# Two places for weight chunks and one more place in each ring of gathered expert rows

## The reference

```python
mod = silu(c) @ w_ada + b_ada                      # shift, scale, gate, twice
h = rmsnorm(x, g1) * (1 + scale1) + shift1
proj = h @ w_in                                    # q k v u gv gate_a gate_b, 7 x 1024 columns
out_b = stick_breaking_attention(q, k, v)          # 8 heads of 128
out_a = u * chunk_spatial_gate(layernorm(gv))
x = x + gate1 * ((gate_a * (out_a @ w_ba) + gate_b * (out_b @ w_bb)) @ w_out)
h = rmsnorm(x, g2) * (1 + scale2) + shift2
# PEER: 8 heads, the best 16 of 16384 experts each
q = h @ w_query
experts, gates = top16_pairs(q @ sub_keys)         # 8 * 16 experts a token
act = gelu(sum(h * expert_down[experts]))
x = x + gate2 * sum(gates * act * expert_up[experts])
y = rmsnorm(x, g_final)
```

## Time and profile before

| | |
|---|---|
| median of 3 runs | 2391.7 us (2390.11 to 2401.53) |
| profiled execution | 2380.01 us, span 2377.8 us |
| PE, TensorE matmuls | busy 1856.2 us, 78% |
| DVE, VectorE | busy 1558.0 us, 66% |
| POOL, GpSimd | busy 1263.7 us, 53% |
| ACT, ScalarE | busy 559.9 us, 24% |
| moved | 844.90 MB, mean 355 GB/s; 604.05 MB of it gathered |

### The profile page before, as it was taken

How to read it: one execution, slowest core, us unless ns; L and a number is a source line. 1 busy time by engine, 2 the same in 40 slices (tenths; PEclk the granted TensorE clock), 3 DMA queues, 4 the chain that set the end, 5 groups by cost and what they waited for, 6 DMA issues and landing times.

```text
span 2377.8 us, 24899 instructions
## 1 busy us (share of the span) xinstructions
PE 1856.2 (78%) x7896; PEld 1296.7 (55%) x7896; DVE 1558.0 (66%) x3451; ACT 559.9 (24%) x1186; POOL 1263.7 (53%) x1169
## 2 busy tenths in 40 slices
PE   4785879888898786998977999778466567777777
PEld 2555878676777564765754577666344223222232
DVE  1210155778888667776787876767679987676662
ACT  1040021476211122136322310111111212122121
POOL 0000025656665455664676665655467677767773
PEclk7997979888999887999977876989688899999999
DMA  7875879998999889996999999999899999999997
GB/s 265 343 274 161 296 292 362 410 348 291 353 388 410 327 324 364 410 412 250 386 408 409 380 401 361 401 380 351 294 410 333 356 358 410 392 409 409 409 409 268
DMA packets 219009, 844.90 MB, mean 355 GB/s; under 512 B 26495, under 2 KB 35639, under 8 KB 197376
## 3 DMA queue, kind: packets, MB, share of 16 engines
q0 software_dynamic: 165888, 604.05, 65.7%
q1 hardware_dynamic: 36820, 216.87, 24.0%
q10 hardware_dynamic: 16172, 22.39, 2.7%
HBM read 826.16 MB, written 16.80 MB: 355 GB/s over the span
## 4 chain that ended last, share of the span: by engine, by line
PE 38%; DMA 21%; DVE 17%; POOL 7%; issue 7%; DVEq 5%; ACT 3%; SPq 1%; ACTq 0%; POOLq 0%
PE bank L846 11%; DMA gather_ring<-in_expert_down,expert_numbers 9%; PE bank L837 9%; PE bank L1202 7%; DVE gather_ring L1920 4%; DVE expert_sums L1951 4%; DMA gather_ring<-in_expert_up,expert_numbers 4%; DMA weight_chunks<-in_w_in 3%; POOL gather_ring L802 3%; POOL gather_ring L787 3%; PE bank L1126 2%; SPq L693 1%; PE bank L1123 1%; DMA weight_chunks<-in_w_ada 1%; POOL weight_chunks L787 1%
## 5 line engine op out<-in xcount | busy, mean ns | idle before, releaser
L787 POOL DMA_INDIRECT gather_ring<-in_expert_down,expert_numbers x510 | 590.0, 1157 | 778.1 <-DVEq L1883 363.3
L1202 PE MATMUL bank<-gather_ring,coef_diagonals 128*128 128x512 f32 x1040 | 578.7, 698 | 264.6 <-DMA gather_ring<-in_expert_up,expert_numbers 155.9
L802 POOL DMA_INDIRECT gather_ring<-in_expert_up,expert_numbers x532 | 564.0, 1060 | 274.1 <-issue 135.1
L1920 DVE CUSTOM_DVE_ANT_0 gather_ring<-gather_ring,h_tiles 128x1024 f32<-128x1024 f32 x410 | 500.1, 1226 | 187.1 <-DMA gather_ring<-in_expert_down,expert_numbers 167.5
L1202 PEld LDWEIGHTS bank<-gather_ring,coef_diagonals 128*128 128x128 f32 x1040 | 213.8, 219 | 561.3 <-issue 402.1
L846 PE MATMUL bank<-hT,weight_chunks 128*128 128x128 f32 (+2 forms) x2304 | 412.4, 341 | 30.4 <-DVE u_and_gv L1773 9.8
L846 PEld LDWEIGHTS bank<-hT,weight_chunks 128*128 128x128 f32 x2304 | 382.0, 202 | 79.8 <-issue 48.8
L1951 DVE SCALAR_TENSOR_TENSOR expert_sums<-gather_ring,expert_coefs,expert_sums 128x1024 f32<-128x1024 f32 x269 | 345.8, 1285 | 8.6 <-issue 8.6
L837 PE MATMUL bank<-weight_chunks,hT 128*128 128x256 f32 x960 | 219.3, 387 | 18.7 <-DMA weight_chunks<-in_w_in 18.2
L837 PEld LDWEIGHTS bank<-weight_chunks,hT 128*128 128x128 f32 x960 | 185.4, 195 | 54.6 <-DMA weight_chunks<-in_w_in 22.7
L1512 ACT ACTIVATE coef_diagonals<-identity,expert_coefs 128x128 f32<-128x128 f32 x304 | 108.3, 395 | 375.4 <-DVE expert_coefs L1931 178.6
(11 more groups left out here) (266 smaller groups left out, 2055.2 us busy)
## 6 DMA issues: line engine op xcount, KB each, us to landing
weight_chunks<-in_w_in SPq DMA_DIRECT2D x84, 1024.0 KB
weight_chunks<-in_w_ada SPq DMA_DIRECT2D x24, 1024.0 KB
weight_chunks<-in_w_query SPq DMA_DIRECT2D x24, 1024.0 KB
weight_chunks<-in_w_branch_a SPq DMA_DIRECT2D x12, 1024.0 KB
weight_chunks<-in_w_branch_b SPq DMA_DIRECT2D x12, 1024.0 KB
weight_chunks<-in_w_out SPq DMA_DIRECT2D x12, 1024.0 KB
gather_ring<-in_expert_up,expert_numbers POOLq DMA_INDIRECT x532, 11.0
weight_chunks<-in_cache_k SPq DMA_DIRECT2D x16, 512.0 KB
```

The costliest lines, as they stand in the source:

```text
L787: pool.indirect_dma_start(out=d_row(slot), out_offset=None, in_=down, in_offset=bass.IndirectOffsetOnAxis(ap=expert[:, t, h * TOPK + k:h * ...
L802: pool.indirect_dma_start(out=u_row(slot), out_offset=None, in_=up, in_offset=bass.IndirectOffsetOnAxis(ap=expert[:, t, h * TOPK + k:h * T ...
L1202: mm = nc.tensor.matmul(bank[6 + half], diag[:, n % 8, :], u_row(slot)[:, half * 512:(half + 1) * 512], start=(u == PE_TILE[t][0]), stop=( ...
L1920: nc.vector.tensor_tensor_reduce(out=row, in0=row, in1=x, scale=1.0, scalar=0.0, op0=ALU.mult, op1=ALU.add, accum_out=dots[:, m % 2, k:k + ...
```

## The change

`weight_chunks` gets two places instead of three (16 KB a partition instead of 24), `gather_ring` thirteen instead of eleven (52 KB instead of 44): six for down and seven for up rows. The sum stays the same. The late rings keep eight places each; two down rows instead of three lie in `weight_chunks` then, and one up row instead of two in `v_tokens`. All indices, waits and counts follow from the three numbers.

```diff
@@ -90,8 +90,8 @@
-D_EARLY, D_LATE = 5, 8
-U_EARLY, U_LATE = 6, 8
+D_EARLY, D_LATE = 6, 8
+U_EARLY, U_LATE = 7, 8
 LATE = 25
@@ -203,7 +203,7 @@
-NW = 3
+NW = 2
```

## The result

The changed kernel takes 2468.4 us (median of 4 runs, 2461.9 to 2484.9) against 2390.9: slower by 77.5 us, ratio 1.0319, 95% interval 1.0274 to 1.0363. The prediction had 2423 and a range to 2460. The profiled execution took 2468.1 us, with a span of 2465.9.

The account below looks back on a forecast made before the run. First stage bound by alternating weight transfers and products, 345 to 1860 us by DMA. Terms 49.5 + 9 + 5 - 4 - 30 + 2 = +31.5 us on the profiled 2380.0 give 2411.5; the median, 11.7 higher, 2423; range 2398 to 2460.

Parts of the forecast that it names:

- (a): First stage, eight ada chunks alone: the eighth ends at 38.8 us instead of 36.9, +2 us.
- (e): End of front 0: four out chunks +2.1 us; queries lose 0.3 us each behind the first gather, counted as nothing.
- (b): q, k and v of front 0: 8.7 us a pair of w_in and ada chunks, 98 us against 69.5, +28.6.
- (d): Merge of front 0: one chunk fewer ready at the modulation store, then 4.33 us a chunk instead of 3.58, +12.5 us.
- (f): First stage, TensorE's clock falling in idle time: slow w_in chunk in half the pairs, +9 us, ends 0 and 27.
- (c): gv and u of front 0: gv 3 would wait, +3 us, and four u chunks add 1.3, +4.3 us.
- Second stage, two places: Fronts 1 and 2: PE falls about 14 us behind, but DMA is the bound; +5 us, ends 0 and 15.
- rival 2: Front 1: PE becomes the bound, its 14 us of weight waits reach the end; 20 for 5, 2438 us, chance 0.05.
- Second stage, rings: Gathers beside fronts 1 and 2: one more place per ring shortens stretches and shallower dips, -30 us, ends -8 and -60.
- ten stops: Stretches between 353 and 1709 us with DVE held up, 48 us in all; each shortened by at most 2.56 us, 24 together.
- The table B2: Near 1671 us, SP asks for this table behind one query chunk instead of two; -4 us, ends 0 and -7.
- The switch to eight places: At row 400, POOL's up gather waits for row 399's sum instead of row 396's; +2 us, ends 1 and 8.

Follow-up runs that it names:

- w2_busy_pe: Kernel before with two weight places, rings five and six, plus ten extra unread matmuls behind each ada chunk in front 0's q, k, v: 2477.5 us against 2391.7.
- w2_alone: Kernel before with two weight places instead of three throughout, rings left at five and six: 2489.7 us against 2391.7.
- w2_front0_only: Kernel before with two weight places for front 0's 72 chunks, three from chunk 72 on, rings five and six: 2468.7 us against 2391.7.
- w2_later_only: Kernel before with three weight places in front 0, two from chunk 72 on, rings five and six: 2414.6 us against 2393.3.
- rings_4_5: Kernel before with one place less in each gather ring (four and five), three weight places: 2416.6 us against 2391.5.

## Why the prediction was wrong

The direction, and front 0 as the place of the loss, were right; the size was not: 31.5 us forecast, 77.5 measured.

**First stage, steps (a) to (e), 49.5 us: right, some 52 measured.** The eighth ada chunk started at 36.86 us, 1.8 later than in the earlier trace rows, with +2 forecast, in part by luck: the first began at 10.44 us, where the term starts from 14.0. Step (b) without the clock is w2_busy_pe: 99.1 us where I had 98. From the end of u to the end of merge it is 13.0 us more, with 12.5 forecast, and the out chunks cost 2.3 for 2.1. The time from issue to use stayed at 4.9 us, and merge chunks took 4.35 us each against 4.33. The idle time at the store began one product earlier: 31.11 us against 26.26. That row lengthens by the one chunk that no longer lay ready, as (d) had it.

**(f), the clock, 9 us: mis-sized.** It measured 19 us in the change's profile: 16 in the eleven pairs of q, k and v (115.1 us against 99.1 in w2_busy_pe), 1.6 at the twelfth chunk and 1.6 at gv 3. I had let half of the pairs run a slow w_in chunk; all eleven did, at 5.1 to 5.5 us. Each had stood behind 3.6 to 5.1 us of idle time, where the two rows that I weighed, had 2.12 and 2.78 before them, and neither was as long as the 3.9 us that I had worked out for the pair. A row that was as long stood in the trace of before, and I didn't use it. Behind 4.09 us of idle time, with 4.6 us of matmuls ahead of that, the four u chunks took 16.41 us, and the granted clock was 0.69 over the first 5.4 us of them (timeline, then window):

```profile
169.07 16.41 PE L846 MATMUL bank<-hT,weight_chunks 128*128 128x128 f32 x128 [4.09 <-DMA weight_chunks<-in_w_in]
...
169.07:174.50 5.43, 5.43 (x34) 5.43 (x35) 3.21 (x6) 0.28 (x1) 0.00 (x0) 0.69 0.75 317
```

It says that every pair would fall. The Trainium skill, "TensorE: Matmul & The Clock Gate", section on HAM oscillation, has the case (a product shorter than the wait, the half rate at every tile), and by that rule (f) was 27. The trace agrees with it in that each pair fell, though with its ada chunk a pair had 4.8 us of work at the full rate, more than its wait. The 27 was too high: I had priced an ada chunk at the lower clock too, and that part (0.85 of 2.45 us a pair) didn't come. In the rows it takes 1.05 us each time, behind the long chunk.

**gv:** step (c) took waits alone. From the start of gv 0 to the end of u it is 7 us more than before, not 4.3; 1.6 of that is gv 3, a slow chunk now (5.2 us instead of 3.62). gv 0 and the start of u were slow in the kernel before already.

**Second stage, two places, +5 (0 to 15): the step that failed most.** Measured 21 us, by w2_alone against w2_front0_only and by w2_later_only. I said that PE's 14 us of waits would be hidden because DMA is the bound there. PE's waits ahead of weight chunks rose by 43 us, not 14, to 55.0 in 32 waits: 30 more of 1.4 us each, where I had 18 of 0.5 to 1. And a share near 1 is no cover: w2_alone moved 356 GB/s instead of 367 over 475 us, which is 14 us. That was rival 2 (chance 0.05), at the right size. Its way, DVE's front pieces waiting for PE, is not what the rows show, though. From 405 to 1950 us DVE's waits for PE's front results are 70 us in both runs; its waits in all are 359 us in w2_alone and 332 in w2_front0_only, and what rose most is its wait for key scores, ahead of the choice of experts, and one wait for the x rows of the residual, which stand behind the chunks in SP's queue (w2_front0_only first, then w2_alone):

```profile
DVE top_values L1836 <- DMA key_scores<-key_scores: 24.5, 5, 8.2
840.64 0.42 DVE L1808 TENSOR_TENSOR scratch_row<-bank,row_tables 128x256 f32<-128x256 f32 x1 [0.72 <-DMA u_and_gv<-in_x_prompt]
...
DVE top_values L1821 <- DMA key_scores<-key_scores: 39.5, 6, 9.8
850.41 0.42 DVE L1793 TENSOR_TENSOR scratch_row<-bank,row_tables 128x256 f32<-128x256 f32 x1 [7.17 <-DMA u_and_gv<-in_x_prompt]
```

The x rows I had named and put inside the 0 to 15. The wait for key scores varies from profile to profile (11.7 us in rings_4_5 to 34.8 with three places later, 39.5 to 53.6 with two), and that it comes from PE's late queries is my reading; no run shows it.

The queries of front 0 under the first gathers, which (e) put at nothing, were 7 us on PE's path into front 1. They aren't part of the 21: w2_front0_only has two places for them as well, and still takes 2055.4 us from its first gather.

**Second stage, rings, -30 (-60 to -8): about right in size, wrong in mechanism.** It measured 21 and 26 us. I had it from ten stops, each shortened by one event. Not one that I looked at is shorter. My reading of why: ahead of a stop the ring is full in both kernels, so what POOL can still issue is what has been freed, and that doesn't depend on the depth. In the stop of 14 us the rows agree: ahead of the last six gathers before it POOL had waited for a place, 2.52 us with rings of five and six and 4.36 with six and seven. Nor was it DVE that held POOL in this stop, as the prediction had it for all ten, but TensorE's sum of an up row. What the extra place does buy is in the shallow dips, which I had given 6 of my 30 us: DVE's waits for down rows fall from 158.3 to 126.6 us. How much of that reaches the end isn't shown.

**The table B2, -4: right in order, no gain to be seen.** In the profile after, the table is asked for behind one query chunk and DVE waits 1.50 us for it, not 4.52, but the stop at the second norm of front 2 lasts about as long as before (9 us at a share of 0.16, 8 at 0.13 before), for DVE waited 8.90 us for the sample tile's tables behind it, and 9.13 before:

```profile
1777.05 1.22 DVE L1810 TENSOR_TENSOR h_tiles<-h_tiles,row_tables 128x1024 f32<-128x1024 f32 x1 [1.50 <-DMA row_tables<-mod_prompt]
...
1790.11 1.28 DVE L1808 SCALAR_TENSOR_TENSOR h_tiles<-u_and_gv,norm_stats,row_tables 128x1024 f32<-128x1024 f32 x1 [8.90 <-DMA row_tables<-mod_sample]
```

**The switch to eight places, +2: right.** POOL waits 3.34 us for the sum of row 399, where the earlier trace rows show 0.30:

```profile
1994.16 0.94 POOL L802 DMA_INDIRECT gather_ring<-in_expert_up,expert_numbers  x1 [3.34 <-PE bank L1202]
```

Put together by what each term measured: 77 + 21 - 26 comes to 72 us, against 77.5. (With the 21 us that the rings gave beside two places it is 77 by construction, and proves nothing.) No single term takes the sum out of the range, which ended 69 us above the median before: with the clock at its end of 27 and the second stage at its end of 15 the sum would be 59.5. But the 21 us of the second stage lie beyond its end, the rings gave 21 to 26 and not 30, the table's 4 us aren't to be seen, and front 0 cost 77 and not 58.5. All these misses went the same way.

## What to carry to other kernels

A prefetch place is worth what its load takes from issue to use, less the other places' work. Here a load took 4.9 us and a product 3.7, so two places passed two chunks in 8.7 us where their products take 7.2, and a pair of a long and a short chunk in 8.7 where its products take 4.8; the idle time in between let TensorE's clock fall as well, and a pair took 10.3. Ask for each buffer in which stage it is scarce: here the ring lay idle just where weight places were short, and lending it (six places in front 0, later three) won 18 us where trading it for good lost 77. And a DMA share near full (0.95 here) didn't cover two places in the later fronts: they cost 21 us.

## What the runs showed of the hardware

A w_in chunk behind 3.6 to 5.1 us of idle time ran at a mean granted clock of 0.68 and took 5.1 to 5.5 us instead of 3.8, in each of eleven pairs of the change, and 2.5 us of matmuls that nothing reads in each pair kept the clock at 1.00 throughout. In the change's q, k and v the next w_in chunk was in use 4.8 to 5.0 us after its issue ten times of eleven, and 6.3 us once; the stretch moved 208 GB/s. The slices near 410 GB/s all lie in the stage with gathers, where several transfers are in flight. A deeper gather ring left stops of 14 and 8 us as long as they were, and still raised the rate of the stage from 365 to 369 GB/s.
